# Score matmuls of the samples: two samples' keys and queries stacked on 128 partitions

## What is computed

```python
qg = q.reshape(b, t, N_KV_HEADS, N_HEADS // N_KV_HEADS, D_HEAD)
s = jnp.einsum('btngd,btjnd->btngj', qg, k_g) * (D_HEAD ** -0.5)
s = jnp.where(valid[:, :, None, None, :], s, -jnp.inf)
p = jax.nn.softmax(s, axis=-1)
o = jnp.einsum('btngj,btjnd->btngd', p, v_g)
```

## Time and profile before

| | |
|---|---|
| median of 3 runs | 1538.35 us (1538.27 to 1539.69) |
| the profiled execution's own time | 1538.17 us |
| its span, first to last instruction | 1536.4 us |
| TensorE busy | 1524.7 us (99%) |
| VectorE, ScalarE, GpSimd busy | 1024.3, 666.6, 454.8 us (67%, 43%, 30%) |
| granted TensorE clock, mean | 0.999 of full speed |
| line 789, records and median duration | 64, 379 ns |
| units of the GLU projection | about 398 to 529 us of the span |

### The profile page before, as it was taken

The page is one execution under the profiler, slowest core; times in us unless marked ns, Lnnn a source line. Parts: engine busy times, 40 slices in busy tenths (PEclk is TensorE's granted clock), DMA queues, the critical chain, the costliest instruction groups (busy, mean ns, idle before and its releaser), DMA issues.

```text
span 1536.4 us, 33763 instructions
## 1 busy us (share of the span) xinstructions
PE 1524.7 (99%) x12448; PEld 1509.3 (98%) x12448; DVE 1024.3 (67%) x1477; ACT 666.6 (43%) x901; POOL 454.8 (30%) x584
## 2 busy tenths in 40 slices
PE   8999999999999999999999999999999999999998
PEld 8999999999999999999999999999999999999998
DVE  7655789888666676567676777777777764444443
ACT  6344345554666544444333333333333333333332
POOL 8992468867323101221111111111111100001100
PEclk9999999999999999999999999999999999999999
DMA  8896477777766586565454545454545475555552
GB/s 267 239 210 184 145 210 209 203 210 195 234 219 200 161 206 210 166 214 175 154 177 151 178 150 179 149 181 148 183 147 185 146 224 176 175 174 174 167 179 94
DMA packets 300222, 282.16 MB, mean 184 GB/s; under 512 B 35280, under 2 KB 292832, under 8 KB 300000
## 3 DMA queue, kind: packets, MB, share of 16 engines
q1 hardware_dynamic: 283968, 256.70, 55.7%
q10 hardware_dynamic: 13840, 16.62, 3.5%
q0 software_dynamic: 2320, 7.54, 1.5%
HBM read 266.73 MB, written 14.05 MB: 183 GB/s over the span
## 4 chain that ended last, share of the span: by engine, by line
PE 88%; DVE 0%; ACT 0%; issue 0%
PE banks L581 28%; PE banks L583 28%; PE banks L582 28%; PE banks L591 1%; PE banks L776 0%; PE banks L817 0%; PE banks L726 0%; PE banks L789 0%; PE banks L713 0%; PE banks L830 0%; PE banks L735 0%; PE banks L638 0%; DVE wlo L1327 0%; PE banks L900 0%; DVE t L1520 0%; ACT yo L1309 0%
## 5 line engine op out<-in xcount | busy, mean ns | idle before, releaser
L1327 DVE TENSOR_TENSOR wlo<-raw,whi 128x1024 fp32r<-128x1024 f32 x443 | 560.1, 1277 | 286.1 <-ACT whi L953 281.8
L953 ACT ACTIVATE whi<-raw 128x1024 fp32r<-128x1024 f32 x443 | 462.4, 1051 | 549.5 <-PE banks L583 492.1
L582 PE MATMUL banks<-h_lo,whi 128*128 128x288 f32 x1408 | 415.7, 295 | 0.0
L583 PE MATMUL banks<-h_hi,wlo 128*128 128x288 f32 x1408 | 415.7, 295 | 0.0
L581 PE MATMUL banks<-h_hi,whi 128*128 128x288 f32 x1408 | 414.6, 294 | 0.0
L581 PE MATMUL banks<-hhi,whi 128*128 128x288 f32 (+1 forms) x912 | 271.1, 297 | 3.6 <-DVE hlo L1353 3.3
L583 PE MATMUL banks<-hhi,wlo 128*128 128x288 f32 (+1 forms) x912 | 269.1, 295 | 0.0
L582 PE MATMUL banks<-hlo,whi 128*128 128x288 f32 (+1 forms) x912 | 269.0, 295 | 0.0
L582 PEld LDWEIGHTS banks<-h_lo,whi 128*128 128x128 f32 x1408 | 264.6, 188 | 0.1
L583 PEld LDWEIGHTS banks<-h_hi,wlo 128*128 128x128 f32 x1408 | 264.4, 188 | 0.0
L581 PEld LDWEIGHTS banks<-h_hi,whi 128*128 128x128 f32 x1408 | 264.1, 188 | 0.1
(11 more groups left out here) (356 smaller groups left out, 2153.5 us busy)
## 6 DMA issues: line engine op xcount, KB each, us to landing
raw<-in_w_up SPq DMA_DIRECT2D x352, 256.0 KB, 3.4
raw<-in_w_in SPq DMA_DIRECT2D x223, 256.0 KB, 3.4
raw<-in_w_down SPq DMA_DIRECT2D x176, 256.0 KB, 3.0
raw<-in_w_glu SPq DMA_DIRECT2D x64, 256.0 KB, 3.5
raw<-in_w_out SPq DMA_DIRECT2D x64, 256.0 KB, 3.3
raw<-in_w_attn_proj SPq DMA_DIRECT2D x32, 256.0 KB, 4.0
scratch_gates<-gt ACTq DMA_DIRECT2D x16, 288.0 KB, 4.4
gbt<-scratch_gates POOLq DMA_DIRECT2D x8, 288.0 KB, 3.5
```

Of the source, the lines that this page charges most:

```text
L582: pe.matmul(out, h, xl[:, kt, :], start=False, stop=False)
L583: mm = pe.matmul(out, lo, xh[:, kt, :], start=False, stop=kt == nk - 1)
L953: act.activation(whi[:, s, :, 0:cols], raw[:, s, :, 0:cols], ACT.Copy).then_inc(hi_ready, 1)
L1327: dve.tensor_tensor(wlo[:, s, :, 0:cols], raw[:, s, :, 0:cols], whi[:, s, :, 0:cols], ALU.subtract).then_inc(lo_ready, 1)
```

## The change

Keys and queries of a pair are stacked: sample 0 of the pair has partitions 0 to 63, sample 1 has partitions 64 to 127, and even and odd heads stand side by side in the free dimension (`kst`, `qst`). A head's scores of both samples are then one matmul of 128 rows, with no second one that adds. There are 4 matmuls a pair. The four transfers of keys carry the same 128 KB each, onto 64 partitions instead of 128. GpSimd makes 8 copies a pair on 64 partitions, for each sample and each half of the heads one of queries and one of new keys; where half and sample differ, the copy goes from one half of the partitions to the other. After each it waits for it to be done. Ahead of the first it waits for its earlier copies of the prompt's operands (for pair 3 also of its values). Both samples' new keys of pair 0 are now staged together, since `kst` does not lie where `kTb[1]` did; `vs` and `spare` have moved to other places.

```diff
-    vs = at("vs", [P, 2, P], F32, WK + 40064)
-    kTb = [at(f"kTb{i}", [P, NPR, SK], F32, (WK + 41088, GR)[i]) for i in range(2)]
-    qbs = at("qbs", [P, NPR, 2, 32], F32, WK + 43168)
+    vs = at("vs", [P, 2, P], F32, WK + 39168)
+    kst = at("kst", [P, NPR, 2, SK], F32, WK + 40192)
+    qst = at("qst", [P, NPR, 2, 32], F32, WK + 44352)
...
                 for b in range(2):
                     for g, page in enumerate(pages(2 * j + b)):
-                        sp.dma_start(kTb[b][:, :, P * g:P * (g + 1)], I["cache_k"][ds(page, 1)].rearrange("a (p q) s -> q (a p) s", p=NPR)
+                        heads = I["cache_k"][ds(page, 1)].rearrange("a (h d) s -> d (a h) s", d=DH)
+                        sp.dma_start(kst[DH * b:DH * (b + 1), :, :, P * g:P * (g + 1)].rearrange("d p n s -> d (p n) s"), heads
                                      ).then_inc(sem("k_in"), 16)
...
                 pe.wait_ge(sem("k_in"), 64 * j + 64)
-                pe.wait_ge(sem("new_ready"), 4 * j + 4)
+                pe.wait_ge(sem("new_ready"), 8 * j + 8)
                 if j:
                     pe.wait_ge(sem("atts_done"), j)
-                for b in range(2):
-                    for p in range(NPR):
-                        for n in range(2):
-                            r, h = slice(DH * n, DH * (n + 1)), 2 * p + n
-                            mm = pe.matmul(aux[32 * h:32 * h + 32, 3, 0:SK], qbs[r, p, b, :], kTb[b][r, p, :], start=b == 0, stop=b == 1)
+                for p in range(NPR):
+                    for n in range(2):
+                        h = 2 * p + n
+                        mm = pe.matmul(aux[32 * h:32 * h + 32, 3, 0:SK], qst[:, p, n, :], kst[:, p, n, :], start=True, stop=True)
                 mm.then_inc(sem("ss_t"), 1)
...
-            def new_keys(i):
-
-                copy(kTb[i % 2][:, :, PAST:SK], kT[:, :, TP + DS * i:TP + DS * (i + 1)]).then_inc(sem("new_ready"), 1)
+            staged = [0]
+
+            def crossing(out, a, rows):
+
+                copy(out, a, ones[rows, 0:1]).then_inc(sem("new_ready"), 1)
+                staged[0] += 1
+                pool.wait_ge(sem("new_ready"), staged[0])
+
+            def new_keys(i, n):
+
+                b, r = i % 2, slice(DH * n, DH * (n + 1))
+                crossing(kst[DH * b:DH * (b + 1), :, n, PAST:SK], kT[r, :, TP + DS * i:TP + DS * (i + 1)], r)
 
             def stage_sample(j):
 
+                pool.wait_ge(sem("unit_staged"), 4 * j if j else 2)
+                if j == 3:
+                    pool.wait_ge(sem("vs_ready"), 2)
                 for b in range(2):
                     i = 2 * j + b
-                    copy(qbs[:, :, b, :].rearrange("p a (g b t) -> p a g b t", g=4, b=2)[:, :, :, b, :],
-                         qT[:, :, TP + DS * i:TP + DS * (i + 1)].rearrange("p (a g) t -> p a g t", a=2)).then_inc(sem("new_ready"), 1)
-                    if i != 1:
-                        new_keys(i)
+                    for n in range(2):
+                        r = slice(DH * n, DH * (n + 1))
+                        crossing(qst[DH * b:DH * (b + 1), :, n, :].rearrange("p a (g b t) -> p a g b t", g=4, b=2)[:, :, :, b, :],
+                                 qT[r, :, TP + DS * i:TP + DS * (i + 1)].rearrange("p (a g) t -> p a g t", a=2), r)
+                        new_keys(i, n)
...
-                    own.link(pool.memset(qbs[:, :, :, :], 0.0))
+                    own.link(pool.memset(qst[:, :, :, :], 0.0))
...
             pool.memset(pTb[:, 2, :], 0.0).then_inc(sem("new_cleared"), 1)
-            new_keys(1)
             z_out(pool, NUT - 1)
```

More of the change, by code:

```diff
@@ L235, in hybrid_decoder_step_kernel @@
     vnew = [at(f"vnew{i}", [P, KV], F32, GR + 8192 + 1024 * i) for i in range(2)]
-    spare = at("spare", [P, 8], F32, WK + 43680)
+    spare = at("spare", [P, 8], F32, WK + 44864)
     maskb = [at(f"maskb{i}", [P, SK], F32, GR + 10240 + 1056 * i) for i in range(2)]
@@ L1876, in copy @@
             def copy(out, a, by=None):
-                one = ones[:, 0:1] if by is None else by
+                one = ones[0:out.shape[0], 0:1] if by is None else by
                 for k in range(len(out.shape) - 2):
```

## The result

The changed kernel takes **1540.78 us** (median of 22 executions, 1538.12 to 1546.11), the kernel before 1538.51 us on the same chips (22 executions, 1537.71 to 1541.22). The ratio is 1.0013, with an interval from 1.0008 to 1.0019: slower by about 2.3 us. That lies within the 0.2% that I had called no change, but the interval excludes no change, and 1540.78 is outside my range. The profiled execution took 1540.65 us, its span is 1538.8 us, 2.4 us longer than before.

The account below looks back on a forecast made before the run. TensorE, busy 1524.7 of 1536.4 us, was taken to bound the kernel; 0.45 us saved on each of four pairs, 1.8 us, off the profiled 1538.17 gave 1536.4 us, range 1535.6 to 1538.6.

Parts of the forecast that it names:

- TensorE's part: Pair's score matmuls: two waves in place of four save 0.45 us a pair, 1.8 us for four pairs.
- rival 2: Scores: weight loads stop overlapping at full height, saving only 0.34 us a pair, 1536.8 us in all; chance 0.09.
- rival 3: Scores: full-height strips take turns at 260 columns, 0.9 us more a pair, 1541.8 us in all; chance 0.04.
- rival 4: Scores: the change does not halve the waves, four stay and nothing is gained, 1538.2 us; chance 0.02.
- GpSimd's part: Staging a pair: eight copies take 2.7 to 3.5 us, at most 10.7; nothing reaches TensorE.
- I charge nothing: Key transfers: even twice the issue and landing times leave 5 us before the scores, so no cost.
- It holds: Unit 0's transposes of the probabilities: TensorE's slack of 0.93 us becomes 0.48, so no wait opens.
- Rival 1: A wait of 0.1 to 0.45 us in each even unit eats the saving; all gone, 1538.2 us; chance 0.08.
- 1.8 us less there is carried through to the end: Behind unit 7: weights run ahead of TensorE (492.1 us of waiting for it), so the whole 1.8 us gain survives.

Follow-up runs that it names:

- run 7: Changed kernel with 2 warm-up matmuls instead of 8, 96 early-met waits and split key transfers: 1537.08, repeated 1537.03 us; without the split 1538.25; split alone 1538.55.
- run 3: Kernel before with the second sample's score matmuls left out in each pair, transfers and copies as before: 1539.28 us, ratio 1.0006.
- run 5: Changed kernel with 48 early-met waits before TensorE's first matmul: 1538.17 us; also with first pair's key transfers split: 1537.32; kernel before with the waits: 1538.47.
- run 6: Changed kernel with 2, then 4 warm-up matmuls in place of 8: 1536.70 and 1537.76 us; unaltered twice more: 1540.74 and 1540.77; one execution each.
- run 1: Changed kernel with 16 one-column matmuls (64 instructions) added behind the warm-up as padding: 1539.74 us, ratio 1.0012.
- run 2: Kernel before with the same padding of 16 one-column matmuls: 1544.31 us, ratio 1.0024.
- run 4: Changed kernel padded with 16 one-column matmuls, key transfers in their old form onto 128 partitions: 1539.78 us, ratio 1.0008.

## Why the prediction was wrong

**TensorE's part** was right: 0.43 us a pair was measured, I took 0.45, between bounds of 0.35 and 0.46. Line 684 as the nearest row gave 0.41. Between the first scores and the down projection the four pairs save 1.7 us once nothing eats it (run 7). That two waves last 0.58 us at full height and 0.57 at half height (run 3) excludes rivals 2 and 3 and also rival 4, since eight records make two waves. The rule behind rival 2, from the Trainium skill, "TensorE: Matmul & The Clock Gate", on packing, does not hold here: at full height no row group is left to differ, and nothing was lost.

**GpSimd's part** was right in that it is hidden; eight copies took 3.7 us, a little over the 2.7 to 3.5 I took and far inside the bounds.

**"I charge nothing"** for the transfers failed. I had doubled their issue and landing and asked only whether the keys would still be in time for the scores. They are, by far. What stood behind them in SyncE's queue was not only the next unit's weights, as the prediction put it, but the second chunk of unit 0 itself, which became available 2.7 us later. The issue rose from 0.376 to 0.628 us each, which four times over is 1.0 us, about the 0.94 by which that chunk is issued later (389.80 to 390.74); the other 1.8 us pass between its issue and ScalarE's start, and why they do stays open.

**"It holds"**, the slack of unit 0, failed from that: I took only TensorE's earlier arrival off the 0.93 us and left VectorE's side as it was, though it stands behind the weights. Rival 1 named this wait and its price (0.1 to 0.45 us; 0.34 was measured), but not its cause, and put it in every even unit. In units 2 and 4 the distances to the next scores fell by 0.41 and 0.39 us (32.77 to 32.36, 32.79 to 32.40), so there nothing was eaten. The size varies by execution, from nothing to 1.4 us in those profiled.

**"1.8 us less there is carried through to the end"** is the step that decided the sign. I reasoned with engines and their supplies of data, and had no line for the supply of instructions. Shorter code ahead of the loop moved everything behind it relative to the fetched blocks, and a fetch that had lain inside the loop came to lie right behind its exit: 2.26 us of stall and 1.5 us from half clock. Runs 3, 5 and 6 show this as cause: the stall came with shorter code and the old transfers, went with waits that are already met, and shrank as fewer warm-ups moved the boundary on. The Trainium skill, "Runtime: NRT & Kernel Launch", on the mechanics of instruction fetch, says that instructions come in blocks of 16 KiB, 256 of them, that a crossing is mostly hidden, and that a taken branch out of the window stalls. The trace agrees on blocks and on straight-line code, where in the down projection blocks come every 15 to 19 us with no wait listed; at a loop's exit, where the code falls through, the crossing was not hidden.

Of the forecast 1.8 us, the profiles show 1.7 and the medians 1.15 to 1.5 once both causes are removed (runs 5 and 7).

Open: why the fetch at the exit starts up to 0.9 us earlier in some kernels than in others at the same distance, which makes the stall 1.3 or 2.1 us; why the drop of the clock follows only the longer one, beyond that it is the longer idle time; and why a transfer onto 64 partitions costs more to issue. The changed kernel's spread up to 1546 us is wider than the stall and the wait account for; no execution of that length was profiled. Nor does the drop of the clock seem tied to the stall alone: of the 33 executions of the kernel before that belong to runs 1 to 4, 7 have a mean granted clock of 0.998 and take 1539.2 to 1539.9 us, the other 26 have a median of 1538.4; of the changed kernel's 22, 13 have 0.998 or 0.997 and a median of 1541.6 us, the other 9 one of 1539.3. That speaks for a drop in those of the kernel before too, but no profile shows one.

## What to carry to other kernels

A change that removes work from TensorE can add time: it moves all code behind it. Where an engine runs a loop and then straight-line code, look for a wait for "issue" a few instructions behind the exit, and if one is there, shift the code by instructions that cost nothing ahead of a start that waits anyway. A transfer that gets slower to issue is to be judged by what is queued behind it, not by its own deadline. And an experiment by padding needs its own control: here the padding cost more than the effect, and what it cost hung on when the clock rose.

## What was not expected of the hardware

- Fetching TensorE's next 16 KB of instructions behind a loop exit stalled it by 2.1 us with 10 instructions in hand (1.3 in two other kernels), 0.6 with 26, 0.2 with 34, and not at all when the block held 14 or more instructions of the loop. TensorE went on 2.2 to 2.4 us after the packet's start in all seven.
- After 2.1 us without a matmul, behind more than 500 us of the loop at full clock (731 to 1242 us), the granted clock was 0.50 for 3.4 us in all three profiles of the changed kernel; after 1.3 us without one it stayed at 1.00 in both kernels that show that.
- Score matmuls of 128x32 and of 64x32 with 260 columns cost the same, 0.58 and 0.57 us for eight records.
- Issuing 128 KB in 512-byte pieces took 0.61 to 0.63 us onto 64 partitions and 0.376 us onto 128.
- Sixteen float32 matmuls with one column took 4.0 us in one kernel and 6.8 us in another: their 32 records start 0.11 us apart at the spacing of the full clock and 0.21 us apart before it rises, where records with 288 columns start 0.13 and 0.24 us apart.
